# Routing of a two-layer MoE model: the third token tile turned ahead of the second tile's logits, the turns back to token rows put behind all logits

## The chip, the cores and the metric

The kernel runs on one core of a Trainium2 chip. The metric is device time in microseconds (us), the median over executions of the whole program. Engines: PE is TensorE (matmuls; "PEld" are its weight loads), DVE is VectorE, ACT is ScalarE, POOL is GpSimd, SP is SyncE, which here only issues DMAs.

## The reference, cut to what matters

The model has two layers. Each is a token mixer (mLSTM, then Mamba-2 SSD) and a hierarchical mixture of experts over 384 tokens (128 of a prompt, 256 of a sample) of width 1024. Around the change the reference does this, in each layer:

```
x  = layer_norm(ALPHA * x + gate * mixer(...))
h  = x * (1 + scale) + shift
glog = h @ w_rg + b_rg                    # 4 groups, top 1
elog = einsum('bld,gde->blge', h, w_re)   # 4 experts in each, top 2
combine = one_hot(group) * softmax(top 2) * softmax(group)
a  = silu(h @ w_gate) * (h @ w_up)        # 16 experts, width 256
out = (a * combine) @ w_down
```

The 20 logits of a token (4 for the groups, 16 for the experts) decide which experts it goes to. The kernel computes an expert only for the tokens that chose it, so nothing of the experts' token lists is known before the logits of all 384 tokens are.

## The kernel before, in words

The tokens are three tiles of 128 (`NT` = 3). `x_tok` holds them with tokens on the partitions; `hT` holds the modulated input turned, with the width on the partitions (8 blocks of 128 by 384 tokens), since matmuls over the width need it so. All engines run their own instruction streams, written by hand in program order, with semaphores between them; no scheduler reorders anything. What stands first in PE's code is executed first, and a wait in it holds everything behind it.

Between the mixer and the experts, layer l does the following (`norm` = 2*l).

1. DVE normalizes a tile in two halves of 512 columns (L2222 in `normalize`) and raises `xn_ready` after each.
2. PE turns a tile with `turn_norm`: two groups of four 128x128 transposes from `x_tok` into PSUM (L680). For tiles 0 and 1 this is done inside the mixer's last projection (`norm_steps`); for tile 2 it is done in `moe`.
3. ACT (L1714) modulates the turned blocks into `hT` and raises `h_act`; of tile 2's second half DVE does this (L2256, `h_dve`).
4. PE computes the logits of tile t with `logits(t)`: eight products with the 20 routing columns and a row for the bias (L698, L700), into bank 6. One such product is two records in the trace, so a tile shows as x16. `await_h` makes it wait for the tile's blocks of `hT`. The bank is released to DVE after tile 2's (the last) logits.
5. PE turns each tile of `hT` back to token rows with `turn_back(t)`: two groups of four transposes (L708) into banks that ACT copies to `m_h` (L1722). After every second copy ACT issues a DMA of the tile's rows to `htok` in DRAM (L1725).
6. DVE reads the 60 logit columns (L2307), finds groups and experts, and raises `chosen` with L2327. PE then counts tokens per expert (L725 to L728), and DVE makes selection matrices (L2337) and the order in which experts' weights are fetched; `planned` is raised at L2363. SP waits for `planned` and issues the remaining weights (L1300). PE picks the first unit's tokens from `m_h` by a matmul with a selection matrix (L748, `picked_tokens`), the others are gathered by POOL from `htok` (L1485).
7. The experts run in eight units (`gate_up`, `turn_tokens`, `down`), then a loop over overflow tokens whose experts' weights are loaded last (L852).

The bank that a `claim` takes is given or comes from a rotation: behind `turn_norm` of tile 2, which is given banks 0 and 1, the rotation is set to banks 0 to 4, starting with bank 2.

Of the kernel before, what the change touches and what calls it, by code (L numbers as in the profile page):

```python
# [32 lines left out]
NT = T // P  # L33
# [47 lines left out]
def program(nc, i_, o_):  # L81
    ctx = ExitStack()
    with ctx:
# [278 lines left out]
        def tile_of(ap, t):  # L362
            return ap[:, P * t:P * t + P]
# [167 lines left out]
        def claim(pe, stage, bank=None, evictions=1, freed_at=None):  # L531


            k = stage_n.get(stage, 0)
            stage_n[stage] = k + 1
            if bank is None:
                bank = next_bank[0] % ring_banks[0]
                next_bank[0] += 1
            if occupant[bank]:
                pe.wait_ge(*occupant[bank])  # L540
            occupant[bank] = freed_at or (read(stage), evictions * (k + 1))
            return (stage, k, bank), banks[bank]

        def finish(ins, key=None):
            n_filled[0] += 1
            ins.then_inc(filled, 1)
            if key:
                group[key[:2]] = (key[2], n_filled[0])
# [31 lines left out]
        def _(pe):  # L580
# [93 lines left out]
            def turn_norm(n, t, at=(None, None)):  # L674
                for half in (0, 1):
                    pe.wait_ge(sem("xn_ready"), 6 * n + 2 * t + half + 1)
                    free = (sem("h_dve"), 4 * n + 4) if t == 2 and half else (sem("h_act"), 20 * n + 8 * t + 4 * half + 4)
                    key, ps = claim(pe, "xn", bank=at[half], freed_at=free)
                    for i in range(4):
                        last = nc.tensor.transpose(ps[:, P * i:P * i + P],  # L680
                                                   x_tok[:, t, 512 * half + P * i:512 * half + P * i + P], ident[:, :])
                    finish(last, key)

            def await_h(n, t, k=KD - 1):

                pe.wait_ge(sem("h_act"), 20 * n + 8 * t + min(k, 3 if t == 2 else 7) + 1)
                if t == 2 and k > 3:
                    pe.wait_ge(sem("h_dve"), 4 * n + k - 3)

            def moe(l):  # L690
# [3 lines left out]
                def logits(t):  # L694
                    await_h(norm, t)
                    for k in range(KD):
                        o = (KD * l + k) * 20
                        mm(lg_ps[:, 20 * t:20 * t + 20], tile_of(hT[:, k, :], t), route_all[:, o:o + 20],  # L698
                           start=k == 0, stop=False)
                    last = mm(lg_ps[:, 20 * t:20 * t + 20], ones[0:1, :], route_b[0:1, 20 * l:20 * l + 20],  # L700
                              start=False, stop=True)
                    finish(last, lg_key if t == NT - 1 else None)

                def turn_back(t):
                    for m in range(2):
                        key, ps = claim(pe, "ht")
                        for i in range(4):
                            last = nc.tensor.transpose(ps[:, P * i:P * i + P], tile_of(hT[:, 4 * m + i, :], t), ident[:, :])  # L708
                        finish(last, key)

                lg_key, lg_ps = claim(pe, "logits", bank=6)
                logits(0)
                logits(1)
                turn_norm(norm, 2, (0, 1))
                ring_banks[0], next_bank[0] = 5, 2
                turn_back(0)
                logits(2)
                for t in (1, 2):
                    turn_back(t)

                pe.wait_ge(sem("chosen"), l + 1)
# [354 lines left out]
            def norm_steps(n, rows_at, more):  # L1076

                def at(stage, i):
# [4 lines left out]
                    elif (stage, i) == (2, 9):  # L1083
# [4 lines left out]
            project_back("yA", "down", lambda k, t: [(0, tile_of(a_xc[:, k, :], t))],  # L1088
                         lambda k: pe.wait_ge(sem("gA_ready"), k + 1), norm_steps(0, 2, lambda stage, i: None))
            moe(0)  # L1090
            for t in range(NT):
                turn_norm(1, t)
# [163 lines left out]
            def squares_left(stage, i):  # L1256
                if stage == 0 and first_sq + i < KE:
                    squares(first_sq + i)

            project_back("yB", "out", grid_rows, lambda k: pe.wait_ge(sem("gB_ready"), k + 1),  # L1260
                         norm_steps(2, 5, squares_left))
            moe(1)


# [1486 lines left out]
```

## Time and profile before

| what | value |
|---|---|
| median of 3 runs | 1315.5 us (1310.4 to 1316.56) |
| profiled execution, its own time | 1316.8 us |
| span of that execution in the trace | 1314.5 us |
| PE busy | 1213.3 us (92%) |
| DVE busy | 716.8 us (55%) |
| ACT busy | 375.2 us (29%) |
| POOL busy | 216.1 us (16%) |
| mean clock granted to PE | 0.951 |
| mean DMA rate | 218 GB/s |

The busy times are shares of the span and overlap each other. A high share of PE says that PE's order matters nearly everywhere, not that each of its instructions is on the path that ends last. The 2.3 us between the span and the execution's own time lie around the trace.

### The profile page before, as it was taken

The page shows a single profiled execution, that of the slowest core. Times are in us where ns is not written, and L with a number is a line of the kernel's source. Part 1 is how long each engine was busy: PE and PEld are TensorE (multiplying, and loading weights), DVE is VectorE, ACT ScalarE, POOL GpSimd, SP SyncE. Part 2 cuts the span into 40 slices and gives each one's busy share as a digit, 9 for nine tenths or more (in the row PEclk, how much of TensorE's full clock was granted, in tenths as well). Part 3 has the DMA queues.
Part 4 walks back from the last instruction along what each step waited for, and adds up shares of the span by engine and source line. Part 5 has one row for each costly group of instructions (what it writes and reads, how often), then busy time and mean ns, then how long its engine had stood idle before and what let it go on. Part 6 is the DMA issues. An engine that isn't in the chain of part 4 may idle for free.

```text
span 1314.5 us, 14623 instructions
## 1 busy us (share of the span) xinstructions
PE 1213.3 (92%) x5148; PEld 657.2 (50%) x5148; DVE 716.8 (55%) x1537; ACT 375.2 (29%) x813; POOL 216.1 (16%) x310
## 2 busy tenths in 40 slices
PE   6999989999999799899968899989999999899973
PEld 3555554664556344743324465656666543654321
DVE  0497355333385499541116895457886688452124
ACT  1444332122300000311115353444546310311121
POOL 5121300000010010000413301003333110010401
PEclk9999999889999899799998899999999999799997
DMA  9752003237597386299966532234434699199974
GB/s 380 248 202 80 1 1 117 76 123 213 223 380 238 119 349 243 78 408 425 426 262 258 205 131 66 96 112 156 137 121 150 231 360 407 48 370 419 424 290 144
DMA packets 76452, 286.49 MB, mean 218 GB/s; under 512 B 7660, under 2 KB 19180, under 8 KB 62684
## 3 DMA queue, kind: packets, MB, share of 16 engines
q1 hardware_dynamic: 42128, 185.35, 36.9%
q0 software_dynamic: 16784, 62.54, 13.0%
q10 hardware_dynamic: 17468, 37.67, 7.9%
q8 instruction: 41, 0.67, 0.2%
q14 instruction: 31, 0.25, 0.1%
HBM read 257.11 MB, written 28.43 MB: 217 GB/s over the span
## 4 chain that ended last, share of the span: by engine, by line
PE 65%; DVE 12%; DMA 9%; issue 8%; ACT 4%; SPq 1%; POOL 0%; ACTq 0%; POOLq 0%; DVEq 0%
PE bank L628 21%; PE bank L793 7%; PE bank L648 5%; PE bank L1009 4%; DMA ring<-in_moe_gu 4%; DVE arena L1993 4%; PE bank L1196 3%; PE bank L813 3%; PE bank L1045 2%; DVE arena L2566 2%; PE bank L897 2%; PE bank L939 2%; DMA ring<-in_b_w_out 1%; PE bank L1037 1%; PE bank L1229 1%
## 5 line engine op out<-in xcount | busy, mean ns | idle before, releaser
L628 PE MATMUL bank<-hT,ring 128*128 128x384 f32 x896 | 301.7, 498 | 7.4 <-ACT arena L1611 4.2
L628 PEld LDWEIGHTS bank<-hT,ring 128*128 128x128 f32 x896 | 173.2, 195 | 128.3 <-issue 10.1
L648 PE MATMUL bank<-ring,arena 128*128 128x512 f32 (+1 forms) x512 | 174.6, 606 | 9.0 <-DVE arena L2181 7.2
L1993 DVE SCALAR_TENSOR_TENSOR arena<-arena 128x1024 f32<-128x1024 f32 x112 | 148.3, 1324 | 19.5 <-DMA arena<-in_ada_wT 12.1
L2017 DVE SCALAR_TENSOR_TENSOR arena<-arena,par 128x388 f32<-128x388 f32 x160 | 99.5, 624 | 60.4 <-ACT arena L1611 55.5
L648 PEld LDWEIGHTS bank<-ring,arena 128*128 128x128 f32 (+1 forms) x512 | 72.6, 195 | 101.2 <-issue 86.0
L793 PE MATMUL bank<-arena,hT 128*64 128x512 f32 (+2 forms) x384 | 102.9, 614 | 4.8 <-issue 4.8
L1196 PE MATMUL bank<-hT,ring 128*128 128x384 f32 x256 | 97.6, 507 | 0.8 <-ACT arena L1611 0.8
L1538 POOL TENSOR_TENSOR arena<-arena 128x192 f32<-128x192 f32 x64 | 43.3, 707 | 209.0 <-PE bank L1229 154.2
L1443 POOL DMA_DIRECT2D arena<-in_ada_wT x74 | 39.1, 531 | 234.0 <-DVE arena L1993 227.4
L793 PEld LDWEIGHTS bank<-arena,hT 128*64 128x64 f32 (+2 forms) x384 | 33.2, 141 | 62.1 <-issue 62.0
L2638 DVE TENSOR_TENSOR arena<-arena 128x1024 f32<-128x1024 f32 x32 | 41.7, 1304 | 35.6 <-ACT arena L1883 35.6
L813 PE MATMUL bank<-arena 128*64 128x512 f32 (+2 forms) x272 | 58.3, 597 | 2.7 <-ACT arena L1741 2.7
L2389 DVE TENSOR_TENSOR arena<-arena,bank 128x256 f32<-128x256 f32 x16 | 6.7, 421 | 94.7 <-ACT arena L1737 94.7
L1009 PE MATMUL bank<-ring,arena 128*128 128x512 f32 x128 | 58.2, 614 | 0.0
L1196 PEld LDWEIGHTS bank<-hT,ring 128*128 128x128 f32 x256 | 44.7, 192 | 26.4 <-issue 8.7
L2566 DVE TENSOR_SCALAR arena<-arena 128x128 f32<-128x128 f32 x192 | 49.9, 328 | 4.0 <-PE bank L1229 4.0
L1993 DVE SCALAR_TENSOR_TENSOR arena<-arena,hT 128x1024 f32<-128x1024 f32 x36 | 44.1, 1224 | 4.1 <-DMA arena<-in_ada_wT 3.1
L1879 ACT ACTIVATE arena<-arena 128x768 f32<-128x768 f32 x32 | 27.0, 843 | 66.2 <-DVE arena L2566 66.2
L1485 POOL DMA_INDIRECT arena<-htok,tok_at x16 | 15.2, 950 | 164.9 <-PE bank L779 126.4
L1009 PEld LDWEIGHTS bank<-ring,arena 128*128 128x128 f32 x128 | 25.1, 198 | 31.3 <-issue 31.2
L897 PE MATMUL bank<-arena,hT 128*128 128x512 f32 x48 | 25.5, 696 | 15.2 <-DMA arena<-yg,slots 15.2
(420 smaller groups left out, 1659.5 us busy)
## 6 DMA issues: line engine op xcount, KB each, us to landing
arena<-in_moe_gu SPq DMA_DIRECT2D x50, 1024.0 KB, 13.7
arena<-in_ada_wT POOLq DMA_DIRECT2D x74, 512.0 KB, 6.4
arena<-in_moe_dn SPq DMA_DIRECT2D x28, 1024.0 KB, 14.9
ring<-in_b_w_in SPq DMA_DIRECT2D x40, 512.0 KB, 3.5
ring<-in_a_w_in SPq DMA_DIRECT2D x32, 512.0 KB, 6.9
ring<-in_moe_gu SPq DMA_DIRECT2D x14, 1024.0 KB, 16.0
arena<-acs_rows ACTq DMA_DIRECT2D x32, 384.0 KB, 3.5
yg<-arena ACTq DMA_DIRECT2D x18, 512.0 KB, 8.0
```

The source lines that it names most:

```text
L628: last = mm(keys[j][1][:, 0:T], w[:, k, P * j:P * j + P], hT[:, 4 * half + k, :], start=half == 0 and k == 0, stop=half == 1 and k == 3, s ...
L648: last = mm(keys[t][1][p:p + tokens.shape[1], :], tokens, w[:, j, :], start=k == 0, stop=k == KE - 1, skip_group_check=True)
L793: last = mm(ps[c:c + n, :], m_hg[:, q % 2, P * k + c:P * k + c + n], v3(held, 4)[:, j, :], start=k == 0, stop=k == KD - 1)
L813: last = mm(ps[c:c + n, :], m_aT[:, P * f + c:P * f + c + n], v3(held, 2)[:, f, 512 * h:512 * h + 512], start=f == 0, stop=f == 1)
L897: last = mm(ps[:, :], w_diag[:, t, i, :], m_y[:, i, t, 512 * half:512 * half + 512], start=i == 0, stop=i == 1)
L1009: last = mm(keys[t - 1][1][:, :], a_qT[:, KH * h + 2 * half + j, P * t:P * t + P], w[:, j, :], start=half == 0 and j == 0, stop=half == 1 ...
L1196: last = mm(ps[:, 0:T], v3(w, 4)[:, k % 4, P * (c % 2):P * (c % 2) + P], hT[:, k, :], start=k == 0, stop=k == KD - 1, skip_group_check=True)
L1538: ins = pl.tensor_tensor(out=b_xdt[c % 2][:, d, :, PH * h:PH * h + PH], in0=b_x[:, :, P * c + PH * h:P * c + PH * h + PH], in1=b_col[:, o: ...
L1993: ins = ve.scalar_tensor_tensor(out=products, in0=c_slots[place][i % 4], scalar=1.0, in1=rows[:, v, :], op0=ALU.mult, op1=ALU.mult, accum_ ...
L2017: last = ve.scalar_tensor_tensor(out=dst, in0=src[:, j:j + W_PAD - 2 * PAD], scalar=w(j), in1=dst, op0=ALU.mult, op1=ALU.add)
L2566: ins = ve.tensor_scalar(b_E[:, h, d, P * t:P * t + P], b_row[:, m % 3, h, P * t:P * t + P], b_col[:, at:at + 1], 0.0, ALU.add, ALU.min)
L2638: ve.tensor_tensor(out=e, in0=e, in1=b_cb[:, g % 2, d, :].unsqueeze(1).to_broadcast([P, 2, 512]), op=ALU.mult).then_inc(sem("w_ready"), 1)
```

## The change

In PE's part of `moe`, for both layers, tile 2's `turn_norm` moves ahead of tile 1's logits, and tile 0's `turn_back` moves from before tile 2's logits to behind them. No instruction is added or removed, and the banks taken stay the same.

```
@@ -710,12 +710,11 @@
                 lg_key, lg_ps = claim(pe, "logits", bank=6)
                 logits(0)
-                logits(1)
                 turn_norm(norm, 2, (0, 1))
                 ring_banks[0], next_bank[0] = 5, 2
-                turn_back(0)
+                logits(1)
                 logits(2)
-                for t in (1, 2):
+                for t in range(NT):
                     turn_back(t)
 
                 pe.wait_ge(sem("chosen"), l + 1)
```

The stretch of PE's stream in layer 0, between the mixer's last projection and the count. L698 and L700 are logits, L680 the turn of tile 2 from `x_tok`, L708 turns back from `hT`; [waits ...] names the semaphores that an instruction waits for. Before:

```order
L698 MATMUL bank6<-route_w,hT 128x20 [waits h_act]
L698 MATMUL bank6<-route_w,hT 128x20 x7
L700 MATMUL bank6<-route_b,ones 128x20
L680 MATMUL bank0<-ident,x_tok 128x128 [waits h_act,xn_ready]
L680 MATMUL bank0<-ident,x_tok 128x128 x3
L680 MATMUL bank1<-ident,x_tok 128x128 [waits h_act,xn_ready]
L680 MATMUL bank1<-ident,x_tok 128x128 x3
L708 MATMUL bank2<-ident,hT 128x128 [waits h_act]
L708 MATMUL bank2<-ident,hT 128x128 x3
L708 MATMUL bank3<-ident,hT 128x128 [waits h_act]
L708 MATMUL bank3<-ident,hT 128x128 x3
L698 MATMUL bank6<-route_w,hT 128x20 [waits h_dve,h_act]
```

The first row is tile 1's logits, the last one the beginning of tile 2's. In the changed kernel the same place, from the end of tile 0's logits on:

```order
L700 MATMUL bank6<-route_b,ones 128x20
L680 MATMUL bank0<-ident,x_tok 128x128 [waits h_act,xn_ready]
L680 MATMUL bank0<-ident,x_tok 128x128 x3
L680 MATMUL bank1<-ident,x_tok 128x128 [waits h_act,xn_ready]
L680 MATMUL bank1<-ident,x_tok 128x128 x3
L698 MATMUL bank6<-route_w,hT 128x20 [waits h_act]
L698 MATMUL bank6<-route_w,hT 128x20 x7
L700 MATMUL bank6<-route_b,ones 128x20
L698 MATMUL bank6<-route_w,hT 128x20 [waits h_dve,h_act]
L698 MATMUL bank6<-route_w,hT 128x20 x7
L700 MATMUL bank6<-route_b,ones 128x20
```

The turn of tile 2 with its wait for `xn_ready` now stands directly behind tile 0's logits, and no L708 stands between logits any more. The second place is the one behind tile 2's logits, up to the count that waits for `chosen`. In the changed kernel:

```order
L708 MATMUL bank2<-ident,hT 128x128 [waits h_act]
L708 MATMUL bank2<-ident,hT 128x128 x3
L708 MATMUL bank3<-ident,hT 128x128 [waits h_act]
L708 MATMUL bank3<-ident,hT 128x128 x3
L708 MATMUL bank4<-ident,hT 128x128 [waits yA_read]
L708 MATMUL bank4<-ident,hT 128x128 x3
L708 MATMUL bank0<-ident,hT 128x128 [waits h_act]
L708 MATMUL bank0<-ident,hT 128x128 x3
L708 MATMUL bank1<-ident,hT 128x128 [waits h_dve]
L708 MATMUL bank1<-ident,hT 128x128 x3
L708 MATMUL bank2<-ident,hT 128x128 [waits ht_read]
L708 MATMUL bank2<-ident,hT 128x128 x3
```

Before, the first four of these rows were not here; the eight behind them were, with the same banks and waits. There are now 24 transposes ahead of the count instead of 16.

## Rows read from the trace of the kernel before

**Rows 1.** The page's chain that ended last, shares of the span by engine.
```profile
PE 65%; DVE 12%; DMA 9%; issue 8%; ACT 4%; SPq 1%; POOL 0%; ACTq 0%; POOLq 0%; DVEq 0%
```

**Rows 2.** Timeline, layer 0: start us, us, engine, line, operation, count, [idle before <-releaser].
```profile
521.76 1.00 DVE L2222 TENSOR_SCALAR x_tok<-x_tok,sm 128x512 f32<-128x512 f32 x2
...
522.36 0.88 PEld L680 LDWEIGHTS bank<-ident,x_tok 128*128 128x128 f32 x8 [3.62 <-DVE x_tok L2222]
...
533.46 2.37 PEld L698 LDWEIGHTS bank<-route_w,hT 128*128 128x128 f32 x16
...
534.50 1.00 DVE L2222 TENSOR_SCALAR x_tok<-x_tok,sm 128x512 f32<-128x512 f32 x2
...
536.42 1.57 PEld L680 LDWEIGHTS bank<-ident,x_tok 128*128 128x128 f32 x8
...
537.97 1.72 PEld L708 LDWEIGHTS bank<-ident,hT 128*128 128x128 f32 x8
...
539.91 3.49 PEld L698 LDWEIGHTS bank<-route_w,hT 128*128 128x128 f32 x16 [0.22 <-issue]
...
543.99 3.27 PEld L708 LDWEIGHTS bank<-ident,hT 128*128 128x128 f32 x16
...
549.05 0.21 DVE L2327 TENSOR_TENSOR arena<-arena 128x48 bf16<-128x48 f32 x1
```

**Rows 3.** Windows of layer 0: stretch, length, PE busy, granted clock, DMA share, GB/s.
```profile
534.00:535.00 1.00, 1.00 (x10) 0.86 0.00 0
...
535.00:536.00 1.00, 1.00 (x6) 0.50 0.00 0
...
548.00:550.00 2.00, 0.38 (x9) 0.91 0.79 326
```

**Rows 4.** Timeline, layer 1, the same places.
```profile
1130.89 2.47 PEld L698 LDWEIGHTS bank<-route_w,hT 128*128 128x128 f32 x16
...
1131.81 1.00 DVE L2222 TENSOR_SCALAR x_tok<-x_tok,sm 128x512 f32<-128x512 f32 x2
...
1133.95 1.57 PEld L680 LDWEIGHTS bank<-ident,x_tok 128*128 128x128 f32 x8
...
1135.50 1.72 PEld L708 LDWEIGHTS bank<-ident,hT 128*128 128x128 f32 x8
...
1137.44 3.49 PEld L698 LDWEIGHTS bank<-route_w,hT 128*128 128x128 f32 x16 [0.22 <-issue]
...
1141.51 3.27 PEld L708 LDWEIGHTS bank<-ident,hT 128*128 128x128 f32 x16
```

**Rows 5.** Windows of layer 1, columns as in rows 3.
```profile
1130.00:1134.00 4.00, 4.00 (x27) 0.76 0.00 0
```

**Rows 6.** Timeline, layer 0, behind the choice of the experts.
```profile
551.91 6.98 PEld L748 LDWEIGHTS bank<-arena 128*128 128x128 f32 x48
...
553.47 0.16 DVE L2363 TENSOR_SCALAR plan<-arena 1x12 int32<-1x12 f32 x1
...
554.64 0.36 SPq L1300 DMA_DIRECT2D arena<-in_moe_gu  x1
```

**Rows 7.** Windows of the expert stage of layer 0, every engine, then clock, DMA share.
```profile
560.00:570.00 10.00, 8.66 (x32) 3.18 (x32) 7.43 (x46) 0.13 (x1) 0.95 (x1) 0.83 1.03 402
...
640.00:650.00 10.00, 10.00 (x49) 3.31 (x50) 1.38 (x2) 1.22 (x3) 4.00 (x2) 1.00 1.01 426
```

**Rows 8.** PE's timeline at the overflow loop, layer 0, then layer 1.
```profile
666.14 0.64 PE L852 MATMUL bank<-arena,hT 128*64 128x512 f32 x1 [1.72 <-DMA ring<-in_moe_gu]
...
1263.72 0.64 PE L852 MATMUL bank<-arena,hT 128*64 128x512 f32 x1 [1.86 <-DMA ring<-in_moe_gu]
```

**Rows 9.** Timeline and DMA issues, layer 0: the token rows' way to DRAM and back.
```profile
548.33 0.33 ACTq L1725 DMA_DIRECT2D htok<-arena  x1
...
htok<-arena ACTq DMA_DIRECT2D x3, 512.0 KB, 2.6
...
554.54 1.03 POOL L1485 DMA_INDIRECT arena<-htok,tok_at  x1 [14.90 <-DVE tok_at L2344]
```

More of the change, by code:

```diff
@@ L712, in moe @@
                 logits(0)
-                logits(1)
                 turn_norm(norm, 2, (0, 1))
                 ring_banks[0], next_bank[0] = 5, 2
-                turn_back(0)
+                logits(1)
                 logits(2)
-                for t in (1, 2):
+                for t in range(NT):
                     turn_back(t)
```

## Prediction

> **What bounds the kernel now.** I read first the page's chain of work that ended last, because it says which engine's order can matter at all: PE carries 65% of it [rows 1], so every stretch of PE's stream is suspect. Then I read the timeline of the changed stretch in layer 0 [rows 2] and, beside it, the windows with the clock granted to PE [rows 3]; then the same for layer 1 [rows 4, 5]. There the reader is to see that PE is never idle: tile 1's logits begin at 533.46 and the turn of tile 2 at 536.42, the turn back of tile 0 at 537.97, tile 2's logits at 539.91, the next turns back at 543.99. The reader is also to see that PE's clock goes from full (2.4 GHz) to half (1.2 GHz) on the way: 0.86 in the window from 534, 0.50 in the next. Before that fall PE had done the logits of tile 0, products of only 20 columns each. The clock comes back near 548, after 16 transposes.
>
> Last, I followed what the routing releases. `chosen` comes from DVE at 549.05 [rows 2], `planned` at 553.47, and SP issues the first of the remaining weights at 554.64 [rows 6]. From then on the DMA engines are full: share 1.03 in the window from 560, 1.01 still in that from 640 [rows 7]. At the end of the stage PE waits 1.72 us for overflow weights in layer 0 and 1.86 us in layer 1 [rows 8]. So from SP's first issue on, the stage is bound by DMA, and the routing sets when that stream starts. A microsecond by which all logits are done later is a microsecond of the kernel; PE alone may be late by up to 1.7 or 1.9 us without anyone's notice.
>
> **The change, step by step, layer 0.** All instructions stay, so the sum is one of waits, of what stands ahead of the last logits, and of the clock.
>
> *The new wait.* Tile 0's logits end at 533.46. DVE's normalization of tile 2 starts at 534.50; for tile 0 PE's first transpose came 0.60 us after that instruction's start (521.76 to 522.36) [rows 2]. So the turn can start at 535.10, and PE idles 1.64 us where it now works on tile 1's logits. Behind the waiting turn stand the logits of tiles 1 and 2, all turns back and the count; for them wait DVE (the choice), then SP and POOL. The second half of the tile is ready about 0.5 us after the first (half of the 1.00 us that the pair takes), before the first four transposes, about 0.8 us at half clock, are through: no second wait.
>
> *The turn*: 536.42 to 537.97, 1.55 us at half clock, is taken as it is (at full clock 0.88 for tile 0, less a wait between its halves) [rows 2]. The fall should again come near 534.7, because PE does the same until 533.46 and then less. Turn: 535.10 to 536.65.
>
> *Tile 1's logits*: before 533.46 to 536.42, 2.96 us, because they began at full clock; now wholly at half clock, like tile 2's, which took 539.91 to 543.99, 4.08 us [rows 2]. Cost 1.12 us. They end at 540.73. Tile 2's blocks in `hT` are written meanwhile by ACT and DVE: from the turn's start at 536.42 to the logits that read them at 539.91 that took at most 3.5 us [rows 2], and from 535.10 to 540.73 there are now 5.6.
>
> *Tile 2's logits*: 540.73 to 544.81, against 543.99 before. *The turn back of tile 0*, 537.97 to 539.91, 1.94 us, has left the stretch.
>
> Sum: +1.64 (wait) - 1.94 (turn back gone) + 1.12 (tile 1's logits at half clock) = +0.82 us.
>
> Layer 1 by the same rows [rows 4, 5]: logits of tile 0 end at 1130.89, turn possible at 1131.81 + 0.60 = 1132.41, wait 1.52; turn back gone, 1135.50 to 1137.44, 1.94; tile 1's logits 3.06 before (1130.89 to 1133.95), 4.08 after (1137.44 to 1141.51 is 4.07), +1.02. Sum: +0.60.
>
> *The turns back at the end.* 24 instead of 16 transposes lie between the last logits and `chosen`. 16 take 3.27 us at half clock, 0.204 each [rows 2], so 24 take 4.9: 544.81 to 549.7. `chosen` comes 549.05 + 0.21 + 0.82 = 550.08. They fit with 0.4 us to spare even if the clock stays low; if it rises near 548.4 as before, they end near 549.1. Cost nothing; without this cover the last eight would cost up to 1.6 us a layer. In layer 1 the same distances give the same spare.
>
> Here the Trainium skill (TensorE: Matmul & The Clock Gate, "Part 4: PE-mode transpose") says that transposes do not count as PE busy in the way matmuls do and do not bring full clock. By that rule the turns would all run at half clock and end at 549.7 rather than 549.1, which leaves the sum as it is but takes most of the spare, and so it bears on the chance of a rival below. The row speaks against the rule: the mean clock from 548 to 550 is 0.91 [rows 3], right behind a stretch in which PE had done only 16 transposes.
>
> *The token rows' way to DRAM.* ACT's copies and three DMA issues to `htok` now all come behind the last logits. The last issue was at 548.33 [rows 9], 1.1 us behind PE's last load of the turns (543.99 + 3.27); behind 549.1 to 549.7 it comes between 550 and 551. Issue to landing took 2.6 us, so the rows land by 553.6 at the latest. POOL's first gather was issued at 554.54 for another reason (DVE's list of tokens) and will be at about 555.4 [rows 9]. Hidden; the cover is some 2 us, and without it POOL's first gather would be late by what is missing.
>
> *Behind the choice.* DVE's chain and SP's issue move as a block: +0.82. The picks (48 loads in 6.98 us, partly at half clock) [rows 6] start later against a rise of the clock that need not move, so PE gets back some 0.3 to 0.4 of it; that is within PE's slack and not counted. The DMA stream carries the delay to the end of the stage: +0.82 and +0.60.
>
> **Sum**: 1.4 us on the profiled execution: span 1314.5 to 1315.9, its time 1316.8 to 1318.2. The median of the runs shown is 1315.5, 1.3 below the profiled execution; I put the delta on it: **1316.9 us**, +0.1%.
>
> **Bounds of the unknown.** Where the clock falls relative to the logits is no property of the order alone. If it falls just before tile 1's logits begin, they cost 4.08 before too, and the change gives 1.64 - 1.94 = -0.30 in layer 0 and 1.52 - 1.94 = -0.42 in layer 1. If it falls only behind tile 1's logits, those cost before some 2.1 (half of 4.08 and a little), and the change costs 1.64 - 1.94 + 1.97 = +1.67. So per layer -0.4 to +1.7; I take the profile's own position. Both ends are far inside 0.5% (6.6 us), which is about what a measurement of this kernel can tell from no change: the runs of before alone span 1310.4 to 1316.56.
>
> **The rivals.**
>
> *The exchange pays (no wait, or a cheap one).* What the order seems to offer is 1.94 us a layer off the way to `chosen`: 3.9 us, 1312.9 us on the profile's time, 1311.6 on the median. It needs tile 2 normalized by 533.46; DVE begins at 534.50 [rows 2] because the mixer's last products for it end late, and no step of the change moves those. Only with the fall of the clock early does a gain of 0.7 us in all remain, 1314.8. Chance 0.13.
>
> *The turns overrun `chosen`.* If a transpose costs 0.215 (8 took 1.72 us [rows 2]) and a last one must drain, 24 take 5.2 to 5.5 us and the count waits up to 0.3 us: +0.5 in all, 1317.4. This is what the skill's rule on transposes would come nearest to. Chance 0.1.
>
> *Slower: the clock comes back too late for the picks and the first unit.* The pause between the turns back and the picks stays, but the picks start 0.8 us later and so have done less when the clock could rise. At 0.204 us each all 48 at half clock take 9.8 instead of 6.98 us, +2.8. The window from 560 has PE busy 8.66 us at a mean clock of 0.83 [rows 7]; the same work at half clock would be 8.66 x 0.83 / 0.5 = 14.4, +5.7. With +0.8 and less the slack of 1.7 that is up to +7.6 a layer, 1331 us. It decides the sign of the verdict when over half of this is paid in both layers. Against it: before, the clock came back near 548 behind 16 transposes [rows 3], and 24 stand there now; of the picks only the first few are shifted. The small form of it (the picks alone late, PE's 3.6 less 1.7) gives +1.9 a layer, 1319.3. Chance 0.14 for the small form, 0.03 for the large.
>
> *The forecast*, +0.5 to +2.5 us with the DMA stream started later: chance 0.6.
>
> **How the numbers follow.** The forecast's 1316.9 with the scatter of medians of before (5 us below, 1 above) and the small rivals gives 1310.5 to 1320.5; the large rival is left out. Same 0.93: all cases but the large slow one lie within 2.8 us of the forecast or 3.9 of before. Faster 0.03, only by scatter on top of a paying exchange. Slower 0.04.
>
> **What the changed profile would show.** PE idle for 1.5 to 1.7 us behind tile 0's logits, released by DVE's normalization; tile 1's logits slower than 2.96 us; the last logits' end 0.6 to 0.8 us later relative to that normalization (9.5 us behind its start before, 534.50 to 543.99, and 10.3 after, in layer 0); 24 transposes in a row, through before `chosen`; SP's first weights as much later; the wait for the overflow weights still there. The prediction is wrong if the clock stays at full through tile 1's logits, if PE's wait in the overflow loop vanishes, or if the expert stage absorbs or multiplies the shift.

## The result, and the profile after

The changed kernel takes 1317.13 us (median of 22 runs, 1312.11 to 1320.81), against 1312.71 us for the kernel before in 22 runs (1306.96 to 1321.11). The ratio is 1.0032 with a 95% interval of 1.0017 to 1.0047: slower by 4.2 us, between 2.2 and 6.2. That is within 0.5% of before, but it is three times the 1.4 us of the forecast, which lies below the interval. That the forecast time of 1316.9 us came out close is luck: it stood on a median of three runs, 1315.5, and the 22 runs of before give 2.8 us less, which made up for the loss that was put too small.

The profiled execution has a span of 1315.9 us (1314.5 before) and a time of 1318.91 us (1316.8 before), at a mean granted clock of 0.949 (0.951). The chain that ended last, against [rows 1]:

```profile
PE 62%; DVE 13%; DMA 11%; issue 8%; ACT 4%; SPq 1%; POOL 0%; ACTq 0%; POOLq 0%; DVEq 0%
```

PE's share went from 65% to 62% and DMA's from 9% to 11%: in this execution the chain passes through more waits for transfers. Layer 0 in the timeline of the changed kernel, against [rows 2, 6]:

```profile
530.35 0.29 PEld L700 LDWEIGHTS bank<-route_b,ones 1*128 1x128 f32 x2
...
531.71 1.00 DVE L2221 TENSOR_SCALAR x_tok<-x_tok,sm 128x512 f32<-128x512 f32 x2
532.31 0.88 PEld L680 LDWEIGHTS bank<-ident,x_tok 128*128 128x128 f32 x8 [1.67 <-DVE x_tok L2221]
...
533.15 3.50 PEld L698 LDWEIGHTS bank<-route_w,hT 128*128 128x128 f32 x16
...
537.24 3.49 PEld L698 LDWEIGHTS bank<-route_w,hT 128*128 128x128 f32 x16
...
541.31 4.98 PEld L708 LDWEIGHTS bank<-ident,hT 128*128 128x128 f32 x24
...
546.64 0.10 PEld L725 LDWEIGHTS bank<-arena,before 128*128 128x128 bf16 x1 [0.35 <-DVE arena L2326]
...
551.99 0.36 SPq L1299 DMA_DIRECT2D arena<-in_moe_gu  x1
```

PE ends tile 0's logits at 530.64 and then waits 1.67 us for DVE's normalization of tile 2; the turn of tile 2 starts 0.60 us behind it. Both tiles' logits (533.15 and 537.24) take 3.5 us each. The 24 turns back are through at 546.3, and the count comes at 546.64, held by nothing but `chosen`. Since the mixer ahead took 2.8 us less in this execution (luck, not the change), times are best read from the start of DVE's normalization, 531.71 here and 534.50 in [rows 2]: the last logits end 9.60 us behind it (9.49 before), SP's first weights leave 20.28 us behind it (20.14). The clock, against [rows 3]:

```profile
530.00:534.00 4.00, 2.43 (x18) 0.90 0.00 0
534.00:536.00 2.00, 2.00 (x11) 0.50 0.00 0
...
538.00:540.00 2.00, 2.00 (x11) 0.50 0.00 0
540.00:542.00 2.00, 2.00 (x9) 0.50 0.04 8
```

It is at half from shortly after 533 until about 546.8 (0.79 is the mean of the window from 546 to 548), through the logits of both tiles. Layer 1, against [rows 4]:

```profile
1129.71 0.29 PEld L700 LDWEIGHTS bank<-route_b,ones 1*128 1x128 f32 x2
...
1130.95 1.00 DVE L2221 TENSOR_SCALAR x_tok<-x_tok,sm 128x512 f32<-128x512 f32 x2
1131.55 1.57 PEld L680 LDWEIGHTS bank<-ident,x_tok 128*128 128x128 f32 x8 [1.55 <-DVE x_tok L2221]
...
1133.10 3.54 PEld L698 LDWEIGHTS bank<-route_w,hT 128*128 128x128 f32 x16
...
1137.22 3.49 PEld L698 LDWEIGHTS bank<-route_w,hT 128*128 128x128 f32 x16
```

Here the turn of tile 2 itself is at half clock (1.57 us instead of 0.88), and the last logits end 10.35 us behind the normalization (9.70 before). At the overflow loop, against [rows 8], in PE's timeline and in the window behind it:

```profile
663.62 1.12 PE L851 MATMUL bank<-arena,hT 128*64 128x512 f32 x1 [3.48 <-DMA ring<-in_moe_gu]
```

```profile
663.00:666.00 3.00, 2.38 (x6) 0.50 1.02 429
```

PE waits 3.48 us for the overflow weights instead of 1.72, and the matmuls behind the wait run at half clock: the first takes 1.12 us instead of 0.64. That had not been forecast.

So one execution of each kernel shows +0.1 and +0.65 us at the last logits, and yet 22 runs of each show +4.2 us. What these two traces hide was the question for the experiments.

### The profile page after: what moved, and what is told of

Read it like the earlier page. It is cut to its first block, busy times and chain, and to the rows that moved or that the text cites. A ratio compares the mean times of both kernels' runs of the same rounds, so it can differ in the third digit from the quotient of the medians.

```text
span 1315.9 us, 14623 instructions
## 1 busy us (share of the span) xinstructions
PE 1211.3 (92%) x5148; PEld 655.7 (50%) x5148; DVE 717.4 (55%) x1537; ACT 375.1 (29%) x813; POOL 216.6 (16%) x310
## 4 chain that ended last, share of the span: by engine, by line
PE 62%; DVE 13%; DMA 11%; issue 8%; ACT 4%; SPq 1%; POOL 0%; ACTq 0%; POOLq 0%; DVEq 0%
PE bank L628 18%; PE bank L792 6%; PE bank L648 5%; DMA ring<-in_moe_gu 4%; DVE arena L1992 4%; PE bank L1008 4%; PE bank L1195 3%; PE bank L812 3%; DMA arena<-in_ada_wT 2%; DVE arena L2565 2%; PE bank L1044 2%; PE bank L896 2%; PE bank L938 2%; PE bank L1036 1%; DMA ring<-in_b_w_out 1%
## 5 line engine op out<-in xcount | busy, mean ns | idle before, releaser
L1992 DVE SCALAR_TENSOR_TENSOR arena<-arena 128x1024 f32<-128x1024 f32 x112 | 148.8, 1328 | 17.9 <-DMA arena<-in_ada_wT 10.4
L792 PE MATMUL bank<-arena,hT 128*64 128x512 f32 (+2 forms) x384 | 99.5, 595 | 4.8 <-issue 4.8
L792 PEld LDWEIGHTS bank<-arena,hT 128*64 128x64 f32 (+2 forms) x384 | 32.1, 137 | 59.7 <-issue 59.7
L896 PE MATMUL bank<-arena,hT 128*128 128x512 f32 x48 | 25.3, 690 | 15.0 <-DMA arena<-yg,slots 15.0
```

What stands on the lines that cost most here:

```text
L792: last = mm(ps[c:c + n, :], m_hg[:, q % 2, P * k + c:P * k + c + n], v3(held, 4)[:, j, :], start=k == 0, stop=k == KD - 1)
L896: last = mm(ps[:, :], w_diag[:, t, i, :], m_y[:, i, t, 512 * half:512 * half + 512], start=i == 0, stop=i == 1)
L1992: ins = ve.scalar_tensor_tensor(out=products, in0=c_slots[place][i % 4], scalar=1.0, in1=rows[:, v, :], op0=ALU.mult, op1=ALU.mult, accum_ ...
```

## The experiments

All kernels are the kernel before with one edit in PE's part of `moe`, and all ratios are against the kernel before, with the 95% interval behind them; 8 to 12 runs stand behind each, where nothing else is said. The theories have letters in the expectations: A is the prediction's own account, B has a second loss in the expert stage, C is scatter, and D, formed on the first traces, is that the clock can come back between the logits of tiles 1 and 2. The place that is read in every trace is the end of tile 2's logits, counted from the start of DVE's normalization of tile 2 ("last logits" below).

**One layer each.** The new order in one layer, the old in the other (cut to its form: `if l == 0:` with the new order's calls, `else:` with the old order's; `l == 1` in the second kernel).

Expected of layer 0 alone:

> The new order in layer 0 alone. Theory A (the routing's last logits are later by what the new wait and the half clock cost, and the DMA stream of the experts passes that on): +0.8 us, and between -0.3 and +1.7 by where the clock falls. Theory B (there is a second loss of 2 to 3 us per layer further down in the expert stage, which the changed kernel's one trace shows in the overflow loop: the wait for the overflow weights 3.48 instead of 1.72 us, and the matmuls behind it at half clock): +2.2 us or more, half of the 4.4 measured for both layers, with the overflow loop longer than before in this layer's trace. Theory C (the difference of the two medians is mostly scatter): 0, within 1.5.

Expected of layer 1 alone:

> The new order in layer 1 alone. Theory A: +0.6 us (-0.4 to +1.7). Theory B: +2 us or more, with the overflow loop of layer 1 longer. Theory C: 0. By all three the two single-layer kernels add up to the changed one, since the layers share nothing but the order of the prefetches.

Measured: layer 0 alone 1.0030 (1.0014 to 1.0046), layer 1 alone 1.0011 (0.9991 to 1.0031). They add up to 1.0041, which agrees with 1.0032 within the intervals. The loss of layer 0, 3.9 us (1.8 to 6.0), is clear of zero, so scatter (theory C) does not explain it. It is also above theory A's range, and the overflow loop of that layer is long again (a wait of 3.54 us, half clock behind it), as theory B has it; in layer 1 alone neither shows (a wait of 1.62 us, full clock). The traces gave something more: each of these kernels has one layer with the old order, and there tile 2's logits took 1.94 us (layer 0) and 1.86 us (layer 1), not the 3.49 of [rows 2, 4], and the last logits ended 6.9 and 7.3 us behind the normalization, not 9.5 and 9.7. They are the two layers from which theory D, below, was formed. The profile on which the forecast rests was of an unlucky execution.

**The turn ahead, or the turn back behind, alone.**

```
                 logits(0)
-                logits(1)
                 turn_norm(norm, 2, (0, 1))
                 ring_banks[0], next_bank[0] = 5, 2
+                logits(1)
                 turn_back(0)
                 logits(2)
```

```
                 logits(1)
                 turn_norm(norm, 2, (0, 1))
                 ring_banks[0], next_bank[0] = 5, 2
-                turn_back(0)
                 logits(2)
-                for t in (1, 2):
+                for t in range(NT):
                     turn_back(t)
```

Expected of the turn ahead alone:

> Only the turn of tile 2 moved ahead of tile 1's logits; the turn back of tile 0 stays ahead of tile 2's logits. Theory A: PE has the wait of 1.6 us and the turn back's 1.9 us both ahead of the last logits, so the last logits end 10.3 + 1.9 = 12.2 us behind the start of DVE's normalization of tile 2 (9.5 to 9.7 before): +2.5 us per layer, +5 us in all. Rival (the turn back costs nothing where it stands, as it covers the way of tile 2's blocks into hT): the last logits wait anyway, and the time is that of the changed kernel, +4.4 as measured, at 10.3 us behind the normalization.

Expected of the turn back behind alone:

> Only the turn back of tile 0 moved behind tile 2's logits; the turn of tile 2 stays behind tile 1's logits. Theory that the turn back delayed tile 2's logits by 1.9 us: -1.9 us per layer, last logits 7.6 us behind the start of the normalization. Rival (the turn back filled the time in which ACT and DVE bring tile 2's blocks into hT, which ended at 539.79 before, 0.12 us ahead of the logits): PE idles 1.9 us there instead, the last logits end 9.5 us behind the normalization as before, and the time is that of before within 1 us, apart from what the clock does in the pause.

Measured: the turn ahead alone is 1.0063 (1.0039 to 1.0087), 8.3 us, the slowest of all kernels with the same instructions. Its timeline in layer 0:

```profile
532.26 1.00 DVE L2222 TENSOR_SCALAR x_tok<-x_tok,sm 128x512 f32<-128x512 f32 x2
...
533.71 3.54 PEld L698 LDWEIGHTS bank<-route_w,hT 128*128 128x128 f32 x16
...
537.84 1.57 PEld L708 LDWEIGHTS bank<-ident,hT 128*128 128x128 f32 x8
...
539.39 3.54 PEld L698 LDWEIGHTS bank<-route_w,hT 128*128 128x128 f32 x16
```

Tile 1's logits, the turn back and tile 2's logits all run at half clock, one behind the other; the last logits end 11.3 us behind the normalization in layer 0 and 12.0 in layer 1. The turn back is in the way here, as theory A said (12.2, and not the 10.3 of its rival): it stands between two tiles' logits with nothing to wait for. The time's interval, 5.1 to 11.4 us, lies just above theory A's +5.

The turn back behind alone is 1.0006 (0.9986 to 1.0027). Its timeline in layer 0:

```profile
531.11 1.00 DVE L2221 TENSOR_SCALAR x_tok<-x_tok,sm 128x512 f32<-128x512 f32 x2
...
532.28 1.03 PEld L680 LDWEIGHTS bank<-ident,x_tok 128*128 128x128 f32 x8
...
535.24 3.49 PEld L698 LDWEIGHTS bank<-route_w,hT 128*128 128x128 f32 x16 [1.92 <-ACT hT L1713]
```

PE now waits 1.92 us, in both layers, for ACT and DVE to bring tile 2's blocks into `hT`, where the turn back had stood. The theory that it delayed tile 2's logits falls: with the turn of tile 2 where it was before, the turn back filled a wait and cost nothing. The last logits ended at 8.2 and 9.5 us, not clearly better than before. In these two kernels eight transposes stand between the logits of tiles 1 and 2, and tile 2's logits ran at half clock in all four layers (3.49 to 3.54 us; in the second kernel there is the wait between, too).

**The same kernels again.** A second and a third profile of each:

> The kernel before, unchanged, for a second profile. Theory D (formed on the profiles of the four kernels so far): in the old order the turn of tile 2 and the turn back of tile 0 stand together as 16 transposes between the logits of tiles 1 and 2, and in a share of the executions they bring PE's clock back to full, so that tile 2's logits end about 7 us behind the start of DVE's normalization of tile 2 (6.8 and 7.2 in the two layers with the old order seen last), and about 9.5 in the others (9.5 and 9.7 in the first profile). Expected: each layer at one or the other, and at least one near 7. Theory A: both near 9.5. The time's ratio to the kernel before is 1 within 0.2%.

> The changed kernel, unchanged, for a second profile. Theory D: the new order has only 8 transposes between logits and then 16 of them in a row, the clock stays at half from the fall to the turns back, and the last logits end 9.5 to 10.3 us behind the normalization in both layers, as in the four layers with the new order seen so far (9.6, 9.7, 10.3, 10.3). +3 to +5 us against before. Theory A: the same place, but +1 to +2 us.

> The kernel before once more, for a third profile. Theory D: tile 2's logits at about 1.9 us (full clock) in at least one layer, last logits 6.8 to 9.7 us behind the normalization of tile 2, mean over all old-order layers under 8.5.

> The changed kernel once more, for a third profile. Theory D: tile 2's logits at about 3.5 us (half clock) in both layers, last logits 8.8 to 10.3 us behind the normalization. A layer with both tiles' logits at full clock would count against it.

Measured: the kernel before again 0.9997 (0.9971 to 1.0023), the changed one again 1.0026 (1.0007 to 1.0046), single times 1313.02 and 1316.96 us in the third pair. The kernel before in its second profile, layer 0:

```profile
532.67 1.90 PEld L698 LDWEIGHTS bank<-route_w,hT 128*128 128x128 f32 x16
...
533.71 1.00 DVE L2222 TENSOR_SCALAR x_tok<-x_tok,sm 128x512 f32<-128x512 f32 x2
...
535.16 1.57 PEld L680 LDWEIGHTS bank<-ident,x_tok 128*128 128x128 f32 x8
...
536.71 1.47 PEld L708 LDWEIGHTS bank<-ident,hT 128*128 128x128 f32 x8
...
538.65 1.86 PEld L698 LDWEIGHTS bank<-route_w,hT 128*128 128x128 f32 x16 [0.47 <-issue]
```

```profile
534.00:536.00 2.00, 2.00 (x12) 0.61 0.00 0
536.00:538.00 2.00, 2.00 (x12) 0.54 0.00 0
538.00:540.00 2.00, 1.73 (x16) 1.00 0.02 10
```

The clock falls during tile 1's logits, as in [rows 3], but here it is back at full when tile 2's logits begin; between lie the turn of tile 2 and the turn back of tile 0, 16 transposes with nothing between them. Tile 2's logits take 1.86 us. Over all layers with either order (each one-layer kernel gives one of each), worked out from the timelines:

| order | last logits behind normalization, us, layer 0 | layer 1 | mean | tile 2's logits at full clock |
|---|---|---|---|---|
| old | 9.5, 6.9, 7.2, 8.0 | 9.7, 7.3, 7.0, 7.0 | 7.8 | 5 of 8 |
| new | 9.6, 9.8, 9.1, 9.6 | 10.4, 10.4, 8.9, 10.3 | 9.7 | 0 of 8 |

The first number of each cell is of the first profile. The difference of the means is 1.9 us a layer, 3.8 in all, against 4.2 measured (the two layers do not reach the end of the stage alike; more on that below). It can be split by the same timelines: the new wait +1.6, the turn back gone -1.9, tile 1's logits +1.5, tile 2's logits +1.2, the turn itself -0.3, being more often at full clock. Theory D had expected 9.5 to 10.3 for every layer of the changed kernel again; two came out at 9.1 and 8.9, because the clock fell only during tile 1's logits, but tile 2 never had full clock. In the old order 16 transposes stand between the two tiles' logits, in the new order none does: the eight of the turn stand ahead of tile 1's. That the old order gives the clock this chance and the new one does not is what the runs show; in which layers of an execution the chance is taken the order alone does not decide (5 of 8).

**Transposes into the new wait.** If it is the 16 transposes together that bring the clock back, they can be put together elsewhere, in PE's wait for the normalization: one turn back in the first kernel, two in the second.

```
                 logits(0)
+                turn_back(0, (2, 3))
+                turn_back(1, (4, 5))
                 turn_norm(norm, 2, (0, 1))
-                ring_banks[0], next_bank[0] = 5, 2
                 logits(1)
                 logits(2)
-                for t in range(NT):
-                    turn_back(t)
+                ring_banks[0], next_bank[0] = 5, 6
+                turn_back(2)
```

(The second kernel against the changed one; the edit of `turn_back`, which here takes the banks of its two groups as a second argument, is left out. The first kernel has `turn_back(0)` alone in this place, keeps the rotation, and turns tiles 1 and 2 back at the end.)

> The new order, but the turn back of tile 0 placed in PE's wait for the normalization of tile 2, so that 16 transposes stand in a row ahead of the logits of tiles 1 and 2. Theory D: the 16 transposes keep or bring back full clock for some of the logits behind them in a share of the executions; last logits 6.5 to 10.5 us behind the normalization, the mean under that of the changed kernel, time +0 to +3 us against before. Theory A: only the wait is filled, nothing else moves: the time of the changed kernel less at most 0.5 us, last logits at 9.6 to 10.5.

> The turns back of tiles 0 and 1 both in PE's wait for the normalization of tile 2 (into banks 2 to 5), so that 24 transposes stand ahead of the logits of tiles 1 and 2. Theory D: denser work ahead of the logits, so full clock for more of them; last logits 6 to 9 us behind the normalization, time -2 to +1 us against before. Theory A: the 16 transposes take 1.8 us at full clock and 3.3 at half clock against a wait of 1.6, so the turn of tile 2 is late by 0.2 to 1.7 us: last logits at 10 to 12 us, +3 to +7 us against before.

Measured: with one turn back in the wait 0.9981 (0.9959 to 1.0004), median 1312.05 us; last logits at 10.2 us in layer 0, with both tiles at half clock, and at 5.9 in layer 1, with both at full. With two turns back 0.9956 (0.9937 to 0.9974), median 1308.69 us: faster than both kernels, by 0.26% to 0.63% against before. Both kernels came out faster than theory D expected (+0 to +3 and -2 to +1 us; measured -2.5 and -5.8): its direction was right, its size too small. Its timeline in layer 0, with two of its windows:

```profile
532.70 1.73 PEld L708 LDWEIGHTS bank<-ident,hT 128*128 128x128 f32 x16
...
533.74 1.00 DVE L2222 TENSOR_SCALAR x_tok<-x_tok,sm 128x512 f32<-128x512 f32 x2
534.39 0.91 PEld L680 LDWEIGHTS bank<-ident,x_tok 128*128 128x128 f32 x8
...
535.27 1.86 PEld L698 LDWEIGHTS bank<-route_w,hT 128*128 128x128 f32 x16
...
537.49 1.86 PEld L698 LDWEIGHTS bank<-route_w,hT 128*128 128x128 f32 x16
...
539.70 0.94 PEld L708 LDWEIGHTS bank<-ident,hT 128*128 128x128 f32 x8
```

```profile
534.00:536.00 2.00, 2.00 (x22) 1.00 0.00 0
...
538.00:540.00 2.00, 2.00 (x18) 1.00 0.65 258
```

The 16 transposes fill the wait to 534.43, the turn of tile 2 starts 0.65 us behind the normalization's start, as early as with nothing ahead of it, and the logits of both tiles run at full clock, 1.86 us each. The last logits end 6.0 us behind the normalization in layer 0 and 6.1 in layer 1. Theory A had turns at half clock that overrun the wait, +3 to +7 us; it falls. This is one profile, and by the table one profile is one draw; that the order pays does not rest on it but on the 12 runs. The last logits, at 6.0 instead of 7.8 us, account for 3.6 of the 5.8 us; no trace here isolates the rest, and the interval (3.4 to 8.3 us) leaves room for there being none.

**What a microsecond ahead of the choice is worth.** In the kernel before, tile 2's eight products are computed twice:

```
-                    for k in range(KD):
+                    for i in range(2 * KD if t == NT - 1 else KD):
+                        k = i % KD
                         ...
```

(Left out: the flags by which the second pass overwrites the first.)

> The kernel before, with tile 2's eight logit products computed twice in both layers (the first pass is overwritten by the second). It measures what a microsecond ahead of the choice is worth. If the DMA stream of the experts starts with the routing and bounds the stage: the second pass costs 1.8 us at full clock or 3.5 at half, the last logits end that much later than 7 to 9.7 us behind the normalization, and the time follows one to one: +4 to +7 us, most likely +6, ratio 1.003 to 1.006. If the expert stage had slack for a late routing: under +2 us in the time although the last logits are as late as said.

Measured: 1.0044 (1.0018 to 1.0069), 5.8 us, between 2.4 and 9.1. Its timeline in layer 0:

```profile
540.35 1.73 PEld L709 LDWEIGHTS bank<-ident,hT 128*128 128x128 f32 x8
...
542.29 3.80 PEld L699 LDWEIGHTS bank<-route_w,hT 128*128 128x128 f32 x32 [0.22 <-issue]
```

The 32 records take 3.80 us at full clock, 1.9 more than 16; the last logits end at 8.9 and 9.3 us, 1.8 and 2.3 us above the 7.2 and 7.0 of the second profile of before, in which tile 2's logits had full clock too. Some 4 us come in and 2.4 to 9.1 come out, so the expert stage cannot hide a late routing; that it passes on just what it gets is compatible with the interval, not shown by it.

## Why the prediction was right in its sign and wrong in its size

**The new wait**: 1.64 and 1.52 us forecast, 1.67 and 1.55 measured. Right. **The turn**: taken at half clock; 0.88 us at full in layer 0 of the first profile, 1.57 in layer 1. Right within 0.7 us.

**Tile 1's logits at half clock**: forecast 4.08 us with the bias against 2.96 before. In the traces the eight products of tile 1 take 2.75 to 3.54 us in the new order, in six of eight layers about 3.5; in the old order 1.86 to 1.90 in six of eight and 2.4 to 2.5 in the first profile. With the bias, that is 1.5 us more on average, against the +1.12 and +1.02 of the forecast: too small by 0.4 us, as the profile at hand showed the dearest form of the old order.

**The step that failed** is in the working for layer 0 and in "Bounds of the unknown": tile 2's logits were put at 4.08 us in both orders, and both ends of the bounds only moved the fall of the clock against tile 1's logits. That the clock can come back between the logits of tiles 1 and 2 was not considered, although the argument used the same thing one step later, where 16 transposes had brought it back near 548. In the old order it came back in 5 of 8 layers, in the new order, with no transpose between these logits, in none of 8. Each such case is worth 1.6 us in the eight products and 1.9 with the bias, 1.2 us a layer on average where the forecast had nothing: with the 0.4 us of tile 1's logits, less 0.3 for turns at full clock, that is the difference between the 0.7 us forecast for a layer and the 1.9 measured at the last logits. The sum's form was right (a wait in, a turn back out, logits at a dearer clock); the clock's part was sized from one execution.

**The turn back gone, -1.94 us**: right as arithmetic, but the reading behind it was loose. With the old order it cost nothing, as the kernel with the turn back behind shows; it lay under the way of tile 2's blocks into `hT`. What covers that way in the new order is tile 1's logits.

**The turns back at the end**: 24 transposes in 4.98 and 3.98 us, through before `chosen`. Right. The Trainium skill (TensorE: Matmul & The Clock Gate, "Part 4: PE-mode transpose") says that full clock does not engage for transposes. The runs here speak against it: in the second profile of before the clock went from 0.54 in the window from 536 to 1.00 in that from 538, behind 16 transposes, and with 24 transposes ahead of the logits of tiles 1 and 2 it was at full for both in both layers of the one profile. By the page's rule the kernel with two turns back in the wait would have had to be as slow as the changed one or slower; it is 0.8% faster by the ratios.

**The token rows to DRAM**: hidden, as forecast. In layer 0 the last of the three issues was at 547.36, 2.6 us from its landing, and POOL's first gather at 551.88, released by DVE's list.

**The DMA-bound stage**: from SP's first weights to the end of the wait for the overflow weights it took 111.50 and 111.81 us before, 111.63 and 111.81 after. In 25 of the 26 layers of all thirteen profiles it lies between 110.6 and 112.2 (the other, layer 1 of the turn ahead alone, has 114.2). A late choice is passed on at that point, as forecast, and the kernel with doubled logits agrees. Missed was what follows in layer 0, and it is what the prediction had named as a sign of being wrong: the expert stage multiplies the shift. In the first pair of profiles the last logits of layer 0 are late by 0.1 us, and PE's wait for the gathered results of the combination (the first L897 or L896) ends 2.9 us later, both against the normalization. Before, then after, with the picks (L748, L747) and the first unit's gate and up products (L793, L792) ahead of it:

```profile
551.95 7.14 PE L748 MATMUL bank<-arena 128*128 128x128 f32 x48
...
561.34 8.79 PE L793 MATMUL bank<-arena,hT 128*64 128x512 f32 x32 [1.82 <-issue]
...
687.02 12.87 PE L897 MATMUL bank<-arena,hT 128*128 128x512 f32 x24 [5.81 <-DMA arena<-yg,slots]
```

```profile
549.28 7.22 PE L747 MATMUL bank<-arena 128*128 128x128 f32 x48
...
558.75 7.09 PE L792 MATMUL bank<-arena,hT 128*64 128x512 f32 x32 [1.82 <-issue]
...
687.09 12.08 PE L896 MATMUL bank<-arena,hT 128*128 128x512 f32 x24 [5.80 <-DMA arena<-yg,slots]
```

In three of four layers 0 with the new order PE waits 3.5 us for the overflow weights, and from the end of the wait to the gate rows (L672) it takes 13.6 to 13.8 us; with waits of 1.7 to 2.1 us, in the old order and in the fourth layer of the new, it took 11.1 to 12.5. From the normalization to the end of the wait for the gathered results the old order takes 151.6 us in layer 0 on average and 154.6 in layer 1, the new order 154.8 and 156.7: +3.2 and +2.1, in sum 5.3, which the interval of the measured 4.2 (2.2 to 6.2) holds. Of layer 0's 3.2 us the last logits explain 1.6, the loop about the same; in layer 1 the last logits explain all. That PE falls to half clock while it waits is what the windows show; why it arrives there earlier against the weights in the new order has not been settled. What fits is that the first unit's gate and up products ran at full clock (7.09 us) in every layer with the new order and at about 8.8 in six of eight with the old. In the three layers 0 with the long wait these products and the picks ahead of them took 14.3 us together, in the other five 15.3 to 16.1: PE won time, spent it waiting for the weights, and lost more at the half clock that followed. In layer 1 with the new order the two took 15.1 to 15.5 us and the wait was between 1.3 and 2.6, so this sum is not all of it, and no run here isolates it.

**The rivals**: "the exchange pays" fell: the new wait came as long as forecast, 1.67 and 1.55 us. "The turns overrun" did not occur. The small form of the late clock is near to what happened in its size (+1.9 us a layer), but at another place: at the logits and in the overflow loop, not at the picks, which in the first pair of profiles took 7.2 and 8.1 us against 7.1 before in both layers.

## What to carry to other kernels

Where an order of short products and transposes decides what clock they get, one profile of before is one draw: ask for each costed stretch at which clock it ran, price it at the other one too, and look for everything that could bring the clock back as well as let it fall. A wait of PE can be filled with work that is needed anyway and that nothing waits for; here two tiles' turns back went into the wait that the change had opened, the logits behind them ran at full clock in both layers of the profile, and a loss of 0.3% became a gain of 0.4%. With one turn back there, they ran at full clock in one layer and at half in the other. An operation that seems to delay its successor may only fill the successor's wait; the profile shows it when the successor's data arrive just ahead of its start. And an engine that gets faster ahead of a wait for DMA need not gain; in three of four layers 0 here PE came out of a longer wait at half clock and lost by it.

## What the runs showed of the hardware that had not been expected

PE's records are back to back during the logits, and still the clock goes to half. In the second profile of before, layer 0:

```profile
530.00:534.00 4.00, 4.00 (x32) 1.00 0.00 0
534.00:536.00 2.00, 2.00 (x12) 0.61 0.00 0
```

PE is busy throughout in both windows. What it did ahead of the fall were products with 20 columns.

The executions of one program scatter with the mean granted clock: the changed kernel's run of 1312.11 us has 0.953, its run of 1320.81 us 0.947 and that of 1320.77 us 0.945. Three runs of before had a median 2.8 us above that of 22. For a change worth 4 us, the number of runs decides as much as the reading of the profile.
